# Feed-forward stages of a four-layer block: high weight blocks against both parts of the features in one 512-column product

## The chip, the cores and the metric

One core of one Trainium2 chip. The metric is the device time of one execution in microseconds (us). Engines: PE is TensorE (PEld its weight loads), DVE is VectorE, ACT is ScalarE, POOL is GpSimd, SP is the queue that issues the DMAs. The clock of TensorE has the levels 1.2 and 2.4 GHz.

## The reference, cut to what matters

Two blocks of two layers each run on 256 tokens of width 1024. The change concerns the feed-forward of the first block's two layers, with `D_FF = 2816`:

```python
def swiglu(h, w_in, w_out):
    a, b = jnp.split(h @ w_in, 2, axis=-1)
    return (jax.nn.silu(a) * b) @ w_out

def sandwich(x, mod, g_pre, g_post, fn):
    shift, scale, gate = mod
    h = rms_norm(x, g_pre) * (1.0 + scale[:, None]) + shift[:, None]
    return x + gate[:, None] * rms_norm(fn(h), g_post)
```

`mod` is the conditioning: `silu(c) @ ada_w + ada_b`, split in shift, scale and gate. After each feed-forward comes another mixer (dilated attention after the first, the second block's attention with an S5 scan after the second).

## The kernel before, in words

**Products in two parts.** All weights are float32. A weight piece of 128 x 1024 (512 KB) is split in a high part, rounded to fp32r (`WH`, made by ScalarE in `hi_to`, L1385), and a low part, the rest (`WL`, made by VectorE in `lo_to`, through the helper at L1876). Features are split likewise (`XH`, `XL`). A product is three matmuls, `mm3` (L633): high weight by high features (L634), and two with one low part each (L635, L636); low by low is left out. In the feed-forward's gate and up products the weight block (128x128) is the stationary operand and 256 tokens are the moving one.

**Pieces.** `weight_plan` lists 504 pieces in the order of use. SP loads them into four slots (`NRAW = 4`): piece n + 4 is loaded once piece n has its low part. Split parts have five slots (`NSPLIT = 5`). ScalarE and VectorE work `LOOK = 3` pieces ahead: `filled(u)` on either engine first makes the parts of all pieces up to `u.piece + LOOK` and then waits until TensorE has filled the unit `u`.

**A feed-forward stage** (`gated`) has 11 turns (`NF = 11`); turn i has a gate unit (2 pieces), an up unit (2 pieces), and the 2 down pieces of turn i - 1. A unit is 256 hidden features x 256 tokens, that is one PSUM bank of 512 columns. Piece numbers: the first feed-forward is 28 to 93, the second 134 to 199; in the second, turn i >= 1 has gate 132 + 6i and 133 + 6i, up 134 + 6i and 135 + 6i, down 136 + 6i and 137 + 6i. Gate and up units, and much else, take banks 0 to 3 (`PSA`) in a ring; the down products sum up in the four banks of `PSB`. After a unit, `gate` on ScalarE writes `Silu` of the bank to a buffer, `product` on VectorE multiplies it by the up bank, `high_of` (ScalarE, `GH`) and `low_of_product` (VectorE, `GL`) split the result for the down products.

**What stands beside it.** `ada_plan` and `ada_places` say behind which low part VectorE takes which step of the conditioning (40 steps in the first feed-forward, each 128 x 1024), before which piece TensorE sums over partitions (`ADA_TOTAL`, in `ada_total`, which takes one bank of the ring or two) and when its rows of `ada_w` are loaded. In the second feed-forward VectorE runs one step of `s5_setup` (a generator) behind each low part, from turn 2 on (`meanwhile` in `lo_to`); in turns 7 to 10 ScalarE takes one Abs and two Sin of 128 x 1024 between `gate` and `high_of`; and TensorE transposes small blocks in `s5_blocks` (two banks), which ScalarE copies to `AD`, in turns 5 and 9, between its `gate` and its `high_of`:

```python
for i in range(NF):
    gate(("ffn", 1), i)
    ...
    for k, where, dst in ((0, 5, BT), (1, 9, CTt)):
        if i == where:
            for r in range(2):
                u = ring.uses["s5t", k, r]
                filled(u)
                e.wait_ge(s_adastep.sem, ada_count(95))
                A.frees(e.copy(dst[r], v3(bank(u.b), 4)), u)
    ...
    high_of(("ffn", 1), i)
```

Every engine runs its program strictly in order. The first feed-forward runs from about 175 to 373 us, the second from about 570 to 760.

Of the kernel before, what the change touches and what calls it, by code (L numbers as in the profile page):

```python
# [7 lines left out]
ALU = mybir.AluOpType  # L8
ACTF = mybir.ActivationFunctionType
F32 = mybir.dt.float32  # L10
F32R = mybir.dt.float32r
# [3 lines left out]
P = 128  # L15
# [3 lines left out]
NF = 11  # L19
NRAW = 4  # L20
NSPLIT = 5
LOOK = 3
# [114 lines left out]
PLAN, FIRST = weight_plan()  # L137
# [26 lines left out]
def ada_plan():  # L164


    step, total, end = {}, {}, {}
    at = 1
    for p in range(2, 12):
        n, part = ADA_PARTS[p]  # L170
        if p == 5:
            at = FIRST["ffn", 0] + 2
        if p == 10:
            at = FIRST["att"] + 2
        pieces = {3: (12, 12, 13, 13, 16, 17, 17, 18), 4: (22, 22, 22, 22, 23, 24, 25, 26)}.get(p, range(at, at + 8))
        for k in range(8):
            if 8 * p + k not in ADA_BEHIND_LEVELS:
                step.setdefault(pieces[k], []).append(8 * p + k)
        last = pieces[7]
        if part == 2 and p != 3:  # L180
            last = max(last, FIRST[STAGES[n]] + ROWS_LOADED + 8)
        total[last + 1] = p
        if p != 3:
            end[last + (3 if p < 5 else 4)] = p
        at = last + (4 if p < 5 else 5)
    return step, total, end
# [174 lines left out]
def build(nc, a, out):  # L361
    ctx = ExitStack()
    with ctx:
        def sb(name, cols, dt=F32):
            return ctx.enter_context(nc.sbuf_tensor(name, [P, cols], dt))
# [11 lines left out]
        def sig(name):  # L377
            return Sig(ctx.enter_context(nc.semaphore(name)))

        PSA = ctx.enter_context(nc.psum_tensor("PSA", [P, 2048], F32))  # L380
        PSB = ctx.enter_context(nc.psum_tensor("PSB", [P, 2048], F32))
        XT = sb("XT", 2048)
        XH = sb("XH", 2048, F32R)
        XL = sb("XL", 2048, F32R)
        GHF = plain("GHF", 2048)
        GH = sb("GH", 2048, F32R)
        GLF = plain("GLF", 2048)
# [6 lines left out]
        T2 = sb("T2", 2048)  # L394
# [21 lines left out]
        s_sq, s_t2, s_xl, s_diag, s_mu = (sig(f"s_{n}_made") for n in ("sq", "t2", "xl", "diag", "mu"))  # L416
        s_xn, s_v, s_y, s_upd, s_fin = (sig(f"s_{n}_made") for n in ("xn", "v", "y", "upd", "fin"))
        s_gh, s_gl = sig("s_gh_made"), sig("s_gl_made")
        ring = Ring(0, [sig(f"s_bank{i}_filled").sem for i in range(4)], [sig(f"s_bank{i}_free").sem for i in range(4)])
# [15 lines left out]
            return CT[0:p, at + a0:at + a0 + n]  # L435

        ident, onesd = cst("ident"), cst("onesd")
        xh, xl = v3(XH[:, :], 8), v3(XL[:, :], 8)
        gh, gl = v3(GH[:, :], 8), v3(GL[:, :], 8)
        t2 = v3(T2[:, :], 8)  # L440
        junk, diag = T2[:, :], v3(T2[:, 1792:2048], 2)
# [5 lines left out]
        def bank(b, lo=0, hi=512, p=P, p0=0):  # L447
            t = PSA if b < 4 else PSB
            o = (b % 4) * 512
            return t[p0:p0 + p, o + lo:o + hi]  # L450

        def quarter(t, b):

            return t[:, 512 * b:512 * b + 512]

        def score_at(u, qt):

# [18 lines left out]
        def used(n):  # L476
            stage = sum(1 for x in ends if x <= n)
            if n + 1 in ends:
                return s_y.sem, 4 * (stage + 1)
            return s_used.sem, n + 1 - stage  # L480


        GLB, at = {}, 0
# [4 lines left out]
        STAGE = {n: i for i, n in enumerate(FIRST)}  # L488


        SPLIT = {n: i for i, n in enumerate(x for x in FIRST if x[0] != "moe")}
# [3 lines left out]
        r = Region(AR, 0, ARENA)  # L495
# [28 lines left out]
        r = Region(AR, 0, ARENA)  # L524
# [9 lines left out]
        blk = AR[:, 1024:2048]  # L534
# [9 lines left out]
        r = Region(AR, 0, ARENA)  # L544
# [9 lines left out]
        r = Region(ARR, 0, ARENA)  # L554
# [6 lines left out]
        r = Region(AR, r.at, 15376)  # L561
# [3 lines left out]
        eouts.append((ARR[:, r.at:r.at + 1024], ARR[:, r.at + 1024:r.at + 2048]))  # L565
        eraw = [r.take(1024) for _ in range(NFAR)]

        sm_at = [640]

        def small(n):  # L570
# [33 lines left out]
        s_glua, s_pad, s_conv, s_silu = (sig(f"s_{n}_made") for n in ("glua", "pad", "conv", "silu"))  # L604
        s_md, s_msb, s_mg, s_mh = (sig(f"s_{n}_made") for n in ("mdec", "msb", "mg", "mh"))
        s_open = sig("s_gates_open")
        s_rd, s_ra = sig("s_route_dve"), sig("s_route_act")
        s_s5r = sig("s_s5_read")
        s_ot, s_rx, s_glum, s_em = (sig(f"s_{n}_made") for n in ("ot", "route", "glum", "em"))
# [17 lines left out]
        def _(e):  # L627
            taken = [0]
# [45 lines left out]
            def half_of_features(u, half, stage):  # L674
                n, h, l = piece()
                h, l = v3(h, 4), v3(l, 4)
                for f in range(2):
                    for k in range(4):
                        kk = 4 * half + k
                        if n - FIRST[stage] < 2 and f == 0:  # L680
                            e.wait_ge(s_xl.sem, 8 * SPLIT[stage] + kk + 1)
                        t = mm3(bank(u.b, f * 256, f * 256 + 256), h[:, k, f * P:(f + 1) * P],
                                l[:, k, f * P:(f + 1) * P], xh[:, kk, :], xl[:, kk, :],
                                half == f == k == 0, kk == 7)
                t.then_inc(used(n)[0], 1)

            def features(tag, stage, free=None):
                u = use(tag, fill=used(taken[0] + 1), free=free)
                u.piece = taken[0] + 1
                half_of_features(u, 0, stage)  # L690
                half_of_features(u, 1, stage)

            def column(tag, stage):
                u = use(tag, fill=used(taken[0]))
# [166 lines left out]
            for f in range(8):  # L861
                t = mm(bank(shifts.b, f, f + 1), accs[1][:, f * P:(f + 1) * P], onesd[:, 0:1], False, f == 7, skip=True)
# [12 lines left out]
            for s in range(2):  # L875
                u = use(("pp", s))
                for x in range(2):
                    g = 2 * s + x
# [29 lines left out]
            u = use("cross")  # L908
# [36 lines left out]
            def gated(stage, n, aside):  # L945
                for i in range(n + 1):
                    if i < n:
                        features((stage, "g", i), stage)
                        aside(3 * i)
                        features((stage, "u", i), stage)  # L950
                        aside(3 * i + 1)
                    if i:
                        if i == 1:
                            aside(-1)
                            wait_sums_read(STAGE[stage])
                        for k in range(2):
                            down(2 * ((i - 1) % 2) + k, GLB[stage] + i, i == 1 and k == 0, i == n and k == 1)
                        aside(3 * i + 2)
# [68 lines left out]


            def s5_blocks(at):
                for k, (where, src) in enumerate(((15, lambda r, i: blk[:, r * 512 + i * P:r * 512 + i * P + P]),  # L1030
                                                  (27, lambda r, i: v4(blk, 2, 4)[:, r, i, :]))):
                    if at == where:
                        e.wait_ge(s_s5b.sem, 1 + k)
                        for r in range(2):
                            u = use(("s5t", k, r))
                            for i in range(4):
                                t = e.transpose(bank(u.b, i * P, i * P + P), src(r, i), ident)
                            t.then_inc(u.fill[0], 1)
# [329 lines left out]
        def _(e):  # L1368
# [3 lines left out]
            def act(o, i, f, bias=0.0, scale=1.0, accum=None):  # L1372
                if accum is None:
                    return e.activation(o, i, f, bias=bias, scale=scale)  # L1374
                return e.activation(o, i, f, bias=bias, scale=scale, accum_out=accum)  # L1375
# [144 lines left out]


            def gate(stage, i):
                u = ring.uses[stage, "g", i]
                filled(u)
                if i >= 2:
                    e.wait_ge(s_gl.sem, GLB[stage] + i - 1)
                A.frees(act(tmps[STAGE[stage]][i % 2], v3(bank(u.b), 2), ACTF.Silu), u)

            def high_of(stage, i):
                u = ring.uses[stage, "u", i]  # L1530
                hi_to(u.piece + LOOK)
                e.wait_ge(*u.free)
                if i >= 2:
                    sem, n = used(FIRST[stage] + 6 * (i - 2) + 9)
                    e.wait_ge(sem, n)
                A(e.copy(gh[:, 2 * (i % 2):2 * (i % 2) + 2, :], tmps[STAGE[stage]][i % 2]), s_gh)
# [325 lines left out]
        def _(e):  # L1862
# [12 lines left out]
            def tt(o, i, j, op):  # L1875
                return e.tensor_tensor(o, i, j, op)  # L1876
# [20 lines left out]
            def filled(u):  # L1897
                if u.piece >= 0:
                    lo_to(u.piece + LOOK)
                e.wait_ge(*u.fill)  # L1900
# [328 lines left out]


            def product(stage, i):
                u = ring.uses[stage, "u", i]
                filled(u)
                e.wait_ge(*ring.uses[stage, "g", i].free)
                tmp = tmps[STAGE[stage]][i % 2]
                V.frees(tt(tmp, tmp, v3(bank(u.b), 2), ALU.mult), u)

            def low_of_product(stage, i):
                low_of(GLB[stage] + i + 1, 2 * (i % 2), 2 * (i % 2) + 2, tmps[STAGE[stage]][i % 2])
# [774 lines left out]
```

## Time and profile before

| | us |
|---|---|
| three runs | 1496.88, 1496.77, 1500.34 |
| their median | 1496.88 |
| the profiled execution, its own time | 1494.02 |
| its span | 1492.1 |

```profile
span 1492.1 us, 23619 instructions
```

In profile lines `xN` is the number of instructions, `[... <-...]` the idle time before an instruction and what ended it, and matmul ends are modelled: how often TensorE can start one is read from the starts.

### The profile page before, as it was taken

To read this page: it belongs to the slowest core of one execution; us is meant where nothing else is said; L and a number is where in the kernel's file an instruction comes from. 1 tells how busy PE (TensorE), PEld (TensorE's weight loads), DVE (VectorE), ACT (ScalarE), POOL (GpSimd) and SP (SyncE) were. 2 spreads that over 40 slices of the span, in tenths; PEclk is the share of its full clock that TensorE was granted. 3 is DMA by queue.
4 is the path that set the end of the run, shared out by engine and by line. 5 is a ranking of instruction groups with operands and counts; after the bars stand their busy time and mean duration, and the time that the engine had idled before them with its cause. 6 is when DMAs were issued, how large, how long until landed. Compare 5 with 4: busy or idle time off the path is not lost.

```text
span 1492.1 us, 23619 instructions
## 1 busy us (share of the span) xinstructions
PE 1419.6 (95%) x9122; PEld 1267.0 (85%) x9122; DVE 1153.5 (77%) x1740; ACT 815.3 (55%) x1189; POOL 1.2 (0%) x5
## 2 busy tenths in 40 slices
PE   7989999999999999999999879999999999899997
PEld 7987899899998979999979768777879998787786
DVE  5998876875866646598569887799988966889997
ACT  2432443434443446444675436788866564678884
POOL 0000000000000000000000000000000000000000
PEclk8999999999999999999999999999999999999999
DMA  9983689986565513656734125899953535589992
GB/s 367 341 315 101 219 302 328 334 293 213 184 198 175 179 57 128 198 177 182 208 113 142 57 91 183 312 360 367 378 199 114 162 122 156 196 320 370 357 367 82
DMA packets 184483, 333.81 MB, mean 224 GB/s; under 512 B 13340, under 2 KB 127796, under 8 KB 184372
## 3 DMA queue, kind: packets, MB, share of 16 engines
q1 hardware_dynamic: 184372, 332.31, 64.7%
q8 instruction: 73, 1.20, 0.3%
q14 instruction: 38, 0.31, 0.1%
HBM read 331.18 MB, written 1.09 MB: 223 GB/s over the span
## 4 chain that ended last, share of the span: by engine, by line
PE 79%; DVE 12%; ACT 4%; issue 3%; DMA 1%; SPq 0%; ACTq 0%; DVEq 0%
PE PSA L634 17%; PE PSA L636 16%; PE PSA L635 16%; PE PSA L631 8%; PE PSB L634 6%; PE PSB L635 5%; PE PSB L636 5%; PE PSB L631 4%; DVE WL L1876 2%; DVE T L1876 2%; ACT WH L1385 1%; DVE ACC L1873 1%; DVE AR L1876 1%; ACT T L1375 1%; DMA WR<-hyb_w_in 1%
## 5 line engine op out<-in xcount | busy, mean ns | idle before, releaser
L1876 DVE TENSOR_TENSOR WL<-WR,WH 128x1024 fp32r<-128x1024 f32 x352 | 421.8, 1220 | 121.4 <-ACT WH L1385 120.8
L1385 ACT CAST WH<-WR 128x1024 fp32r<-128x1024 f32 x352 | 354.9, 1048 | 104.1 <-DMA WR<-hyb_w_in 44.9
L634 PE MATMUL PSA<-XH,WH 128*128 128x256 f32 x1312 | 378.7, 289 | 8.5 <-DVE AR L2278 2.5
L635 PE MATMUL PSA<-XL,WH 128*128 128x256 f32 x1312 | 372.6, 284 | 0.0
L636 PE MATMUL PSA<-XH,WL 128*128 128x256 f32 x1312 | 372.6, 284 | 0.0
L634 PEld LDWEIGHTS PSA<-XH,WH 128*128 128x128 f32 x1312 | 253.0, 193 | 13.5 <-issue 5.4
L635 PEld LDWEIGHTS PSA<-XL,WH 128*128 128x128 f32 x1312 | 253.1, 193 | 1.2 <-issue 0.7
L636 PEld LDWEIGHTS PSA<-XH,WL 128*128 128x128 f32 x1312 | 252.8, 193 | 0.0
L1876 DVE TENSOR_TENSOR WL<-AR,WH 128x1024 fp32r<-128x1024 f32 x152 | 178.4, 1220 | 18.8 <-ACT WH L1385 18.6
L634 PE MATMUL PSB<-WH,GH 128*128 128x512 f32 x416 | 164.7, 396 | 3.3 <-DVE GL L1876 3.3
L635 PE MATMUL PSB<-WL,GH 128*128 128x512 f32 x416 | 162.8, 391 | 0.0
L636 PE MATMUL PSB<-WH,GL 128*128 128x512 f32 x416 | 162.8, 391 | 0.0
L1385 ACT CAST WH<-AR 128x1024 fp32r<-128x1024 f32 x152 | 151.4, 1049 | 5.0 <-PE PSA L636 5.0
L634 PE MATMUL PSA<-WH,XH 128*128 128x256 f32 (+1 forms) x352 | 116.1, 330 | 5.5 <-DVE AR L1873 2.7
L1374 ACT ACTIVATE AR<-PSA 128x256 f32<-128x256 f32 (+1 forms) x82 | 37.7, 462 | 143.9 <-PE PSA L636 143.9
L636 PE MATMUL PSA<-WH,XL 128*128 128x256 f32 (+1 forms) x352 | 113.5, 322 | 0.0
L635 PE MATMUL PSA<-WL,XH 128*128 128x256 f32 (+1 forms) x352 | 113.2, 322 | 0.0
L634 PEld LDWEIGHTS PSB<-WH,GH 128*128 128x128 f32 x416 | 78.5, 189 | 22.2 <-issue 6.8
L636 PEld LDWEIGHTS PSB<-WH,GL 128*128 128x128 f32 x416 | 78.5, 189 | 16.8
L635 PEld LDWEIGHTS PSB<-WL,GH 128*128 128x128 f32 x416 | 78.5, 189 | 15.4 <-issue 0.2
L631 PE MATMUL PSA<-CT 128*128 128x256 f32 (+1 forms) x312 | 74.8, 379 | 7.0 <-DMA XT<-x 7.0
L634 PEld LDWEIGHTS PSA<-WH,XH 128*128 128x128 f32 x352 | 67.0, 190 | 11.7 <-DVE AR L1873 2.9
(259 smaller groups left out, 2042.4 us busy)
## 6 DMA issues: line engine op xcount, KB each, us to landing
AR<-moe_w_gate_up SPq DMA_DIRECT2D x96, 512.0 KB, 5.9
WR<-ffn_w_in SPq DMA_DIRECT2D x88, 512.0 KB, 4.5
WR<-moe_w_gate_up SPq DMA_DIRECT2D x64, 512.0 KB, 5.8
AR<-ada_w SPq DMA_DIRECT2D x59, 512.0 KB, 8.6
AR<-moe_w_down SPq DMA_DIRECT2D x56, 512.0 KB, 6.0
WR<-ffn_w_out SPq DMA_DIRECT2D x44, 512.0 KB, 4.3
WR<-att_w_qkv SPq DMA_DIRECT2D x36, 512.0 KB, 4.8
AD<-ada_w SPq DMA_DIRECT2D x34, 512.0 KB, 5.8
```

The costliest lines, as they stand in the source:

```text
L631: return e.matmul(o, l, r, start=start, stop=stop, skip_group_check=skip)
L634: e.matmul(o, lh, rh, start=start, stop=False, skip_group_check=True)
L635: e.matmul(o, lh, rl, start=False, stop=False, skip_group_check=True)
L636: return e.matmul(o, ll, rh, start=False, stop=stop, skip_group_check=True)
L1374: return e.activation(o, i, f, bias=bias, scale=scale)
L1375: return e.activation(o, i, f, bias=bias, scale=scale, accum_out=accum)
L1385: A(e.copy(hi_slot(m), raw_slot(m)), s_hi)
L1873: return e.scalar_tensor_tensor(out=o, in0=i, scalar=s, in1=j, op0=op0, op1=op1)
L1876: return e.tensor_tensor(o, i, j, op)
```

## The change

In all gate units and in the up units of turns 0 to 9, a high weight block meets the high and the low features in one matmul of 512 columns; the low block meets the high features in one of 256, added to the half for small sums. `XH` and `XL` become one tensor, `XHL`. A unit then takes two banks: for each of its two feature blocks, 256 columns of large sums and 256 of small ones. The last up unit keeps three matmuls and one bank. ScalarE copies the small sums out, VectorE adds the large ones; Silu then reads the buffer. ScalarE makes one high part more before it waits for VectorE. In `ada_plan` the steps and sums inside the first feed-forward move back by four pieces (the last by three), and the S5 transposes move from behind the gate unit of turns 5 and 9 (`aside` numbers 15, 27) to behind the down products in the same turns (17, 29).

```diff
 ada_plan:
-            at = FIRST["ffn", 0] + 2
+            at = FIRST["ffn", 0] + 6
...
-        pieces = {3: (12, 12, 13, 13, 16, 17, 17, 18), 4: (22, 22, 22, 22, 23, 24, 25, 26)}.get(p, range(at, at + 8))
+        pieces = {3: (12, 12, 13, 13, 16, 17, 17, 18), 4: (22, 22, 22, 22, 23, 24, 25, 26),
+                  9: (82, 83, 84, 85, 86, 87, 88, 88)}.get(p, range(at, at + 8))
 TensorE:
+            def wide_half(u, half, stage):
+                n, h, l = piece()
+                h, l = v3(h, 4), v3(l, 4)
+                for f in range(2):
+                    large_and_small = v3(bank(u.b + f), 2)
+                    for k in range(4):
+                        kk = 4 * half + k
+                        if n - FIRST[stage] < 2 and f == 0:
+                            e.wait_ge(s_xl.sem, 8 * SPLIT[stage] + kk + 1)
+                        mm(large_and_small, h[:, k, f * P:(f + 1) * P], xhl[:, :, kk, :], half == k == 0, kk == 7, skip=True)
+                        t = mm(large_and_small[:, 1, :], l[:, k, f * P:(f + 1) * P], xh[:, kk, :], False, kk == 7, skip=True)
+                t.then_inc(used(n)[0], 1)
+            def wide_features(tag, stage):
+                u = use(tag, 2, fill=used(taken[0] + 1))
...
-                        features((stage, "g", i), stage)
+                        wide_features((stage, "g", i), stage)
                         aside(3 * i)
-                        features((stage, "u", i), stage)
+                        (wide_features if i < n - 1 else features)((stage, "u", i), stage)
...
-                for k, (where, src) in enumerate(((15, ...), (27, ...))):
+                for k, (where, src) in enumerate(((17, ...), (29, ...))):
 ScalarE, gate:
-                A.frees(act(tmps[STAGE[stage]][i % 2], v3(bank(u.b), 2), ACTF.Silu), u)
+                A(e.copy(tmp, parts_of(u)[1]), s_small)
+                hi_to(u.piece + LOOK + 1)
+                e.wait_ge(*u.free)
+                A(act(tmp, tmp, ACTF.Silu), s_fsil)
 ScalarE, high_of:
                 hi_to(u.piece + LOOK)
-                e.wait_ge(*u.free)
+                if i < NF - 1:
+                    e.wait_ge(*u.fill)
+                    if nth:
+                        e.wait_ge(s_prod.sem, nth)
+                    A(e.copy(up_sum, parts_of(u)[1]), s_small)
+                    hi_to(u.piece + LOOK + 1)
+                    e.wait_ge(s_prod.sem, nth + 1)
+                else:
+                    e.wait_ge(*u.free)
 VectorE, product:
-                filled(u)
-                e.wait_ge(*ring.uses[stage, "g", i].free)
-                tmp = tmps[STAGE[stage]][i % 2]
-                V.frees(tt(tmp, tmp, v3(bank(u.b), 2), ALU.mult), u)
+                filled(g)
+                e.wait_ge(s_small.sem, smalls + 1)
+                V.frees(tt(tmp, parts_of(g)[0], tmp, ALU.add), g)
+                filled(u)
+                if i == NF - 1:
+                    e.wait_ge(s_fsil.sem, nth + 1)
+                    V.frees(tt(tmp, tmp, v3(bank(u.b), 2), ALU.mult), u)
+                else:
+                    e.wait_ge(s_small.sem, smalls + 2)
+                    V.frees(tt(up_sum, parts_of(u)[0], up_sum, ALU.add), u)
+                    e.wait_ge(s_fsil.sem, nth + 1)
+                    V.wait()
+                    V(tt(tmp, tmp, up_sum, ALU.mult), s_prod)
```

## Rows read from the trace of the kernel before

**Rows 1.** The page: busy time by engine, and the chain by engine.

```profile
PE 1419.6 (95%) x9122; PEld 1267.0 (85%) x9122; DVE 1153.5 (77%) x1740; ACT 815.3 (55%) x1189; POOL 1.2 (0%) x5
...
PE 79%; DVE 12%; ACT 4%; issue 3%; DMA 1%; SPq 0%; ACTq 0%; DVEq 0%
```

**Rows 2.** Windows, two turns of each stage: busy us (instructions), clock, DMA share, GB/s.

```profile
241.00:277.00 36.00, 36.00 (x254) 33.64 (x255) 23.18 (x24) 12.95 (x16) 0.00 (x0) 1.00 1.01 348
...
629.60:665.00 35.40, 35.40 (x248) 32.68 (x248) 32.63 (x52) 16.05 (x19) 0.00 (x0) 1.00 0.58 181
```

**Rows 3.** Timeline of TensorE, first feed-forward: start us, us, engine, line, operation.

```profile
209.77 0.28 PE L634 MATMUL PSA<-XH,WH 128*128 128x256 f32 x1
...
217.93 0.28 PE L636 MATMUL PSA<-XH,WL 128*128 128x256 f32 x1
218.05 0.40 PE L634 MATMUL PSB<-WH,GH 128*128 128x512 f32 x1
...
223.29 0.39 PE L636 MATMUL PSB<-WH,GL 128*128 128x512 f32 x1
223.51 0.28 PE L634 MATMUL PSA<-XH,WH 128*128 128x256 f32 x1
```

**Rows 4.** Timeline of TensorE, start of the up unit of turn 6.

```profile
283.86 0.28 PE L636 MATMUL PSA<-XH,WL 128*128 128x256 f32 x1
284.83 0.38 PE L634 MATMUL PSA<-XH,WH 128*128 128x256 f32 x1 [0.69 <-ACT AR L1374]
```

**Rows 5.** Timeline, start of the first feed-forward, ScalarE and TensorE.

```profile
172.38 3.75 ACT L1374 ACTIVATE T<-PSA,MC 128x256 f32<-128x256 f32 x8 [3.21 <-PE PSA L631]
...
175.16 0.36 PE L634 MATMUL PSA<-XH,WH 128*128 128x256 f32 x1
```

**Rows 6.** Timeline of VectorE, second feed-forward, turns 4 and 5.

```profile
640.91 1.22 DVE L1876 TENSOR_TENSOR WL<-WR,WH 128x1024 fp32r<-128x1024 f32 x1
...
649.56 0.68 DVE L1876 TENSOR_TENSOR AR<-AR,PSA 128x512 f32<-128x512 f32 x1
650.93 0.69 DVE L1876 TENSOR_TENSOR GL<-AR,GH 128x512 fp32r<-128x512 f32 x1 [0.69 <-ACT GH L1536]
651.88 1.22 DVE L1876 TENSOR_TENSOR WL<-WR,WH 128x1024 fp32r<-128x1024 f32 x1 [0.26 <-ACT WH L1385]
...
654.28 1.22 DVE L1876 TENSOR_TENSOR WL<-WR,WH 128x1024 fp32r<-128x1024 f32 x1
...
656.67 1.22 DVE L1876 TENSOR_TENSOR WL<-WR,WH 128x1024 fp32r<-128x1024 f32 x1
...
658.53 1.22 DVE L1876 TENSOR_TENSOR WL<-WR,WH 128x1024 fp32r<-128x1024 f32 x1
...
660.84 1.22 DVE L1876 TENSOR_TENSOR WL<-WR,WH 128x1024 fp32r<-128x1024 f32 x1
...
663.44 1.22 DVE L1876 TENSOR_TENSOR WL<-WR,WH 128x1024 fp32r<-128x1024 f32 x1
```

**Rows 7.** Timeline of TensorE, the transposes of turn 5.

```profile
656.62 1.04 PE L1037 MATMUL PSA<-CT,AR 128*128 128x128 f32 x8
657.41 0.36 PE L634 MATMUL PSA<-XH,WH 128*128 128x256 f32 x1
```

**Rows 8.** Timeline of ScalarE, turn 5: the copies of the transposes.

```profile
657.31 1.07 ACT L1590 COPY AD<-PSA 128x512 f32<-128x512 f32 x2
```

**Rows 9.** Timeline of ScalarE, turn 9: Abs and two Sin.

```profile
727.03 2.17 ACT L1374 ACTIVATE AR<-AR 128x1024 f32<-128x1024 f32 x2
729.12 1.13 ACT L1374 ACTIVATE AR<-AR,CT 128x1024 f32<-128x1024 f32 x1
```

**Rows 10.** Windows at a fall of TensorE's clock (columns as in rows 2).

```profile
776.90:780.30 3.40, 1.59 (x19) 1.02 (x18) 2.98 (x4) 2.06 (x6) 0.00 (x0) 1.00 0.13 14
780.30:783.80 3.50, 3.50 (x17) 3.50 (x18) 1.03 (x1) 3.37 (x8) 0.00 (x0) 0.51 0.87 286
```

More of the change, by code:

```diff
@@ L382, in build @@
         XT = sb("XT", 2048)
-        XH = sb("XH", 2048, F32R)
-        XL = sb("XL", 2048, F32R)
+        XHL = sb("XHL", 4096, F32R)
         GHF = plain("GHF", 2048)
@@ L437, in build @@
         ident, onesd = cst("ident"), cst("onesd")
-        xh, xl = v3(XH[:, :], 8), v3(XL[:, :], 8)
+        xhl = v4(XHL[:, :], 2, 8)
+        xh, xl = xhl[:, 0], xhl[:, 1]
         gh, gl = v3(GH[:, :], 8), v3(GL[:, :], 8)
@@ L454, in quarter, with parts_of @@
             return t[:, 512 * b:512 * b + 512]
+        def parts_of(u):
+            return tuple(v4(PSA[:, u.b * 512:u.b * 512 + 1024], 2, 2)[:, :, x] for x in range(2))
         def score_at(u, qt):
@@ L566, in build @@
         eraw = [r.take(1024) for _ in range(NFAR)]
+        up_sum = v3(T2[:, 1024:1536], 2)
         sm_at = [640]
@@ L606, in build @@
         s_open = sig("s_gates_open")
+        s_small, s_fsil, s_prod = (sig(f"s_ffn_{n}_made") for n in ("small", "silu", "product"))
         s_rd, s_ra = sig("s_route_dve"), sig("s_route_act")
@@ L691, in features @@
                 half_of_features(u, 1, stage)
+            def wide_half(u, half, stage):
[12 more added lines that the diff above has]
+                u = use(tag, 2, fill=used(taken[0] + 1))
+                u.piece = taken[0] + 1
+                wide_half(u, 0, stage)
+                wide_half(u, 1, stage)
             def column(tag, stage):
@@ L1029, in s5_blocks @@
             def s5_blocks(at):
-                for k, (where, src) in enumerate(((15, lambda r, i: blk[:, r * 512 + i * P:r * 512 + i * P + P]),
-                                                  (27, lambda r, i: v4(blk, 2, 4)[:, r, i, :]))):
+                for k, (where, src) in enumerate(((17, lambda r, i: blk[:, r * 512 + i * P:r * 512 + i * P + P]),
+                                                  (29, lambda r, i: v4(blk, 2, 4)[:, r, i, :]))):
                     if at == where:
@@ L1522, in gate @@
             def gate(stage, i):
-                u = ring.uses[stage, "g", i]
+                u, tmp = ring.uses[stage, "g", i], tmps[STAGE[stage]][i % 2]
                 filled(u)
@@ L1526, in gate @@
                     e.wait_ge(s_gl.sem, GLB[stage] + i - 1)
-                A.frees(act(tmps[STAGE[stage]][i % 2], v3(bank(u.b), 2), ACTF.Silu), u)
+                A(e.copy(tmp, parts_of(u)[1]), s_small)
+                hi_to(u.piece + LOOK + 1)
+                e.wait_ge(*u.free)
+                A(act(tmp, tmp, ACTF.Silu), s_fsil)
             def high_of(stage, i):
-                u = ring.uses[stage, "u", i]
+                u, nth = ring.uses[stage, "u", i], (NF - 1) * (STAGE[stage] // 2) + i
                 hi_to(u.piece + LOOK)
-                e.wait_ge(*u.free)
+                if i < NF - 1:
[7 more added lines that the diff above has]
+                    e.wait_ge(*u.free)
                 if i >= 2:
@@ L2231, in product @@
             def product(stage, i):
-                u = ring.uses[stage, "u", i]
-                filled(u)
-                e.wait_ge(*ring.uses[stage, "g", i].free)
-                tmp = tmps[STAGE[stage]][i % 2]
-                V.frees(tt(tmp, tmp, v3(bank(u.b), 2), ALU.mult), u)
+                g, u, tmp = ring.uses[stage, "g", i], ring.uses[stage, "u", i], tmps[STAGE[stage]][i % 2]
+                nth, smalls = NF * (STAGE[stage] // 2) + i, (2 * NF - 1) * (STAGE[stage] // 2) + 2 * i
+                filled(g)
+                e.wait_ge(s_small.sem, smalls + 1)
+                V.frees(tt(tmp, parts_of(g)[0], tmp, ALU.add), g)
+                filled(u)
+                if i == NF - 1:
[7 more added lines that the diff above has]
+                    V(tt(tmp, tmp, up_sum, ALU.mult), s_prod)
             def low_of_product(stage, i):
```

## The prediction

> **What bounds the kernel now.** I read the page's first and fourth parts, then the two feed-forward stages stage by stage. TensorE is busy 95% of the span and carries 79% of the chain that ended last, VectorE 12% [rows 1]. So a product saved on TensorE is time saved, provided that the split weight blocks and the PSUM banks still come in time. The windows say where that is in doubt: the first feed-forward's two turns at 241 have VectorE busy 23.2 us of 36, with DMA at its limit, while in the second's two turns at 630 VectorE is busy 32.6 of 35.4 [rows 2]. TensorE hardly waits in either.
>
> **The products.** TensorE starts a matmul of 256 columns every 0.120 us (68 steps in 8.16 us) and one of 512 every 0.228 (23 steps in 5.24); going from 256 to 512 costs 0.12, from 512 to 256 0.22 to 0.23: the cost is that of the earlier matmul [rows 3]. A weight block of 128x128 costs 3 x 0.120 = 0.360 now, and 0.228 + 0.120 = 0.348 afterwards: 0.0125 us less. What goes is one matmul's fixed part, not streaming. There are 21 wide units per stage (11 gate, 10 up) of 16 blocks: 336, two stages 672, so 8.4 us, 4.2 in each stage. No row shows a moving operand in two strips of 256, 2048 columns apart; I take the plain 0.228, its nearest row. The bounds: 0.240 (as two narrow ones: gain 0), and both matmuls at bare streaming, 512/2.4 + 256/2.4 = 0.320 a block (gain 26.9 us).
>
> Here a rule speaks otherwise. The Trainium skill, TensorE: Matmul & The Clock Gate (Back-to-back issue gap), gives N/2.4 + 2.5 ns between matmuls for a single stream; 512 and 256 columns would then take 0.216 + 0.109. By it, with now's 0.360 kept, 672 blocks would save 23.5 us. The trace doesn't agree: beyond streaming it has 13 to 14 ns for either width.
>
> **First feed-forward (pieces 28 to 93).** A unit now needs two of four banks. Gate, up, gate, up use the pairs in turn, so a unit waits for the one two before it, which has 11 us to be read. The moved conditioning sums (pieces 42, 54, 66, 78, 89 in place of 38, 50, 62, 74, 86) come after both units of a turn, so no up unit lands on its own gate's banks. That happens once now, at 283.86: 0.97 us between matmuls, 0.85 of it a wait for ScalarE's Silu [rows 4]. I count -0.85. VectorE gets two additions of 0.69 more per turn, ScalarE two copies of 0.60; of VectorE's 13 us of slack per two turns [rows 2] this takes 2.8, so 0. The conditioning DMAs move four pieces with their sums, on SP past the bias table's load; fewer stand ahead of that load, one or two stand between it and the same weights as before: 0, bounds -1 and +2 (DMA share 1.01). At the stage's start the first gate waits for the features' transposes 5 and 6 to be read, now only for 4. ScalarE's eight reads run from 172.38 for 3.75, so number 6 ends at about 175.7; TensorE started at 175.16 [rows 5]: +0.55, and +0.1 in the second stage, where the ring stands one bank otherwise. First stage: -4.2 - 0.85 + 0.55 = -4.5.
>
> **Second feed-forward (pieces 134 to 199): VectorE's chain.** The S5 set-up runs in steps behind each low split (the line that writes WL). From WL of piece 160 at 640.91 to the end of that of 163 at 653.10 VectorE has only the wait of 0.69 for GH and 0.26 for WH [rows 6]: 12.2 us. Afterwards this stretch has two additions (+1.4), and the 0.26 goes, as ScalarE splits one piece ahead: 13.3. It starts some 1.3 earlier, at 639.6 (TensorE is 1.5 us ahead by gate 3, ScalarE splits 156 directly after its short S5 work, one addition more stands before), and ends at 653.0; bounds 0.8 either way. TensorE wanted piece 163 at 653.74 (656.62 less 24 x 0.12, [rows 7]), a margin of 0.65. By then 21 halves have saved 0.10 each: wanted at 651.65, wait 1.3.
>
> From there VectorE sets the pace. A gate's addition stands behind the low splits up to three pieces on, and Silu waits for it. I step on with 2.40 from a split to the next over a long set-up step, 1.87, 2.31 and 2.60 over others [rows 6], 1.7 over two short ones (estimate), 0.7 for an addition, 2.06 from product to end of GL; TensorE with 2.78 a half unit and 2.73 a down piece.
> - Turn 5: 164 starts at 654.2, 165 at 656.6, 166 at 658.5, gate 5's addition at 660.8, 167 at 661.5, 168 at 664.1. TensorE does 163 from 653.0, is through up 5 at 661.4 and the down products at 666.85. Then the wait at gate 6 (next part); WL 169 ends at 673.1.
> - Turn 6: 170 at 674.3, 171 at 676.7, 172 at 678.6, gate 6's addition 680.9, 173 at 681.6, 174 at 684.2, up 6's addition 686.6, WL 175 ends at 690.6. TensorE, from 673.1, wants it after a half, up 6, two down pieces and a half: 689.7. Wait 0.9.
> - Turn 7: gate 7 is full at 694.1, but its addition comes behind 176, 177 and 178 at 697.5. Now Silu follows TensorE at once; then it starts at 698.2, Abs and two Sin behind it, and high split 180 begins at 701.9. So 181's low split ends at 709.2, wanted at 707.2: wait 2.0.
> - Turn 8: in the same way 1.4 at 186 and 1.1 at 187.
>
> Together 1.3 + 0.9 + 2.0 + 1.4 + 1.1 = 6.7 us.
>
> **The S5 transposes.** They move from pieces 164 and 188 to 168 and 192: from behind gate 5 (and 9) to behind up 5 (9) and the down products. ScalarE's program doesn't move with them. It runs gate(5), then the copies of the transposes, then high_of(5), which now begins with the copy of up 5's small sums. So ScalarE waits for transposes that come after the down products; up 5's copy is queued behind that wait; VectorE waits for the copy; and gate 6 needs the banks of up 5, with nothing between the transposes and it. TensorE's 0.79 us of transposes stands either way [rows 7]. Then it waits for two copies (1.07, [rows 8]), the small copy (half of that and its end, 0.60), the addition (0.68, as the product in [rows 6]) and handoffs (0.25, an estimate), less 0.4 that the first copy overlaps: 2.2 us. Its second piece, WL 169, comes 3.3 later (product, GH, GL in 2.06, a split in 1.22) against a half unit's 2.78: 0.5. In turn 9 Abs and two Sin (3.1, [rows 9]) stand between the copies and the small copy: 2.2 + 3.1 = 5.3, and 0.5 again. Sum 8.5. VectorE idles beside both; the chain above counts that in. Nothing hides these waits, as all other work of TensorE is ordered behind gate 6 and gate 10.
>
> The clock: it fell to 1.2 GHz for 3.5 us (granted 0.51) after a stretch with TensorE busy 1.59 of 3.40 us [rows 10]. A wait of 5.3 is emptier, so I expect one fall: up to 1.7 us, less 0.5 that the late split 193 covers: +1.2, bounds 0 and 3.4 (both waits).
>
> **Sum.** -8.4 - 0.85 + 0.65 + 6.7 + 8.5 + 1.2 = +7.8 us. The profiled execution took 1494.02 (span 1492.1), so 1501.8 by its own time; the median of the runs shown, 1496.88, is 2.86 above it, and I give the result on that: 1504.7 us. The attention stage gets other bank numbers but the same order of reuse: 0.
>
> **Rivals.**
> - Only the S5 waits bite; VectorE's chain keeps its lead (its steps overlap better than I add them). -8.6 + 8.5 + 1.2 = +1.1: 1498. For: they are ordering, not throughput. Against: a margin of 0.65 us and 92% busy. Chance 0.20.
> - Faster: VectorE keeps its lead and the four-bank ring doesn't hold TensorE in turns 5 and 9, because ScalarE's copy of the small sums doesn't wait there as I read it. It decides at gates 6 and 10: if TensorE starts them within 0.3 us of the transposes, only -8.6 is left: 1488. Chance 0.08.
> - The 512 columns cover the next weight load, and only streaming is left: 0.320 a block. The second stage ends by VectorE's chain, which doesn't move, so the first alone gains, 336 x 0.040 = 13.4 in place of 4.2; the waits stay. +7.8 - 9.2 = -1.4: 1495.5. For: the 0.012 beyond streaming at 256 could be the load of 128 columns. Against: the same stands behind 512. Chance 0.07. The gap that the Trainium skill gives on the page above is this case with 11.8 for 13.4.
> - Nothing gained: two strips cost as two matmuls (0.240). Second stage as forecast, first 4.2 worse: +12: 1509. Or DMA holds the first stage or both waits drop the clock: +10 to +12. Chance 0.12.
> - The forecast, +4.5 to +10: 0.53.
>
> **The numbers.** About 0.3%, 4.5 us, is what a measurement of this kernel can tell from no change. Faster by more: the second rival and a little of the third, 0.10. Within: the first, most of the third and the forecast's lower edge, 0.28. Slower: 0.62. The range leaves out the fast case and the worst of the fourth: 1494 to 1511.
>
> **What would show it.** Spacing of 0.228 and 0.120 in turn within a wide unit; no bank wait in the first stage, which ends 4 to 5 us earlier. In the second, low splits just before or after TensorE wants them from turn 5 on; TensorE idle 2.2 us at gate 6 and 5.3 at gate 10, put down to VectorE's addition; a clock drop there. I am wrong if TensorE runs through gates 6 and 10, or if the second stage isn't longer than now.

## The result and the profile after

| us | before | after |
|---|---|---|
| median (lowest to highest), five runs each | 1496.88 (1496.54 to 1500.34) | 1508.56 (1506.52 to 1513.03) |
| the profiled execution, its span | 1494.02, 1492.1 | 1513.03, 1511.2 |
| first feed-forward, first gate product to last down product | 197.93 | 194.95 |
| between the two | 196.72 | 198.12 |
| second feed-forward | 190.33 | 203.45 |
| from there to TensorE's last matmul | 722.73 | 722.68 |

Slower: ratio 1.0074, interval 1.0058 to 1.0089, 11.7 us by the medians; +7.8 was forecast. The stage lengths are worked out from the starts of the TensorE instructions; those of the two feed-forward stages include 0.23 for the last product, the two other rows run from start to start. The first feed-forward gained 3.0 us and the second lost 13.1. The two profiled executions also differ by 7.5 us ahead of the first feed-forward (it starts at 182.69, before at 175.16) and by 1.4 between the two, where the change touches little or nothing; before_again, below, comes back to that. So stages are compared here, not ends of span.

The page of the changed kernel: span, busy times, the chain by engine, and the group of the new product, to be read beside [rows 1].

```profile
span 1511.2 us, 22426 instructions
...
PE 1426.0 (94%) x8450; PEld 1240.5 (82%) x8450; DVE 1179.4 (78%) x1782; ACT 840.0 (56%) x1231; POOL 1.2 (0%) x5
...
PE 66%; DVE 18%; ACT 6%; issue 5%; DMA 4%; SPq 1%; ACTq 0%; DVEq 0%
...
L640 PE MATMUL PSA<-XHL,WH 128*128 128x512 f32 x672 | 241.3, 402 | 12.0 <-DVE T L1917 7.1
```

672 matmuls fewer, and TensorE is no less busy; its share of the chain fell from 79 to 66%, VectorE's rose from 12 to 18%. The group's last numbers are the loss in short: 12 us of idle time before the wide matmuls, 7.1 of it ended by VectorE's addition of the sums.

The timeline of TensorE in the first stage (start, length, instruction) answers to [rows 3], and its lines at 284 to [rows 4].

```profile
217.72 0.40 PE L640 MATMUL PSA<-XHL,WH 128*128 128x512 f32 x1
217.96 0.28 PE L640 MATMUL PSA<-XHL,WL 128*128 128x256 f32 x1
...
222.31 0.40 PE L640 MATMUL PSA<-XHL,WH 128*128 128x512 f32 x1
...
284.72 0.28 PE L640 MATMUL PSA<-XHL,WL 128*128 128x256 f32 x1
285.82 0.50 PE L640 MATMUL PSA<-XHL,WH 128*128 128x512 f32 x1 [0.82 <-DVE WL L1917]
```

From 217.72 to 222.31 are 13 pairs, 353 ns each. Over the whole stage, by the recorded starts, the next matmul starts 234.5 ns behind a wide one and 116.7 behind a narrow one on average, 351 a block (the medians are 233 and 117, but the steps behind a wide one vary from 230 to 241, so the average is what adds up). The wait for a bank is gone, but TensorE waits 0.98 us at 284.72, now for a low part. VectorE's timeline:

```profile
283.93 0.69 DVE L1917 TENSOR_TENSOR GL<-AR,GH 128x512 fp32r<-128x512 f32 x1 [0.69 <-ACT GH L1577]
284.54 1.22 DVE L1917 TENSOR_TENSOR WL<-WR,WH 128x1024 fp32r<-128x1024 f32 x1
```

The high part that this split needs was ready at 282.17 (ScalarE's copy of 1.05 from 281.12); the split stood behind the product and `GL` in VectorE's program.

The timeline at gates 6 and 10, TensorE first. The transposes are L1067; an `xN` line holds N instructions, the last of which start at 673.96 and 749.24.

```profile
673.20 1.04 PE L1067 MATMUL PSA<-CT,AR 128*128 128x128 f32 x8
676.24 0.50 PE L640 MATMUL PSA<-XHL,WH 128*128 128x512 f32 x1 [2.01 <-DVE T L1917]
...
748.47 1.04 PE L1067 MATMUL PSA<-CT,AR 128*128 128x128 f32 x8
754.58 0.80 PE L640 MATMUL PSA<-XHL,WH 128*128 128x512 f32 x1 [5.07 <-DVE T L1917]
755.17 0.42 PE L640 MATMUL PSA<-XHL,WL 128*128 128x256 f32 x1
755.39 0.63 PE L640 MATMUL PSA<-XHL,WH 128*128 128x512 f32 x1
755.82 0.41 PE L640 MATMUL PSA<-XHL,WL 128*128 128x256 f32 x1
756.03 0.63 PE L640 MATMUL PSA<-XHL,WH 128*128 128x512 f32 x1
```

ScalarE and VectorE in the same two places: copies of the transposes (L1631), Abs and Sin (L1404), the copy of the small sums (L1569), then VectorE's addition (L1917, `T<-PSA,T`).

```profile
673.83 1.07 ACT L1631 COPY AD<-PSA 128x512 f32<-128x512 f32 x2 [2.67 <-PE PSA L1067]
674.79 0.60 ACT L1569 COPY T<-PSA 128x512 f32<-128x512 f32 x1
675.50 0.69 DVE L1917 TENSOR_TENSOR T<-PSA,T 128x512 f32<-128x512 f32 x1 [2.98 <-ACT T L1569]
...
749.11 1.07 ACT L1631 COPY AD<-PSA 128x512 f32<-128x512 f32 x2 [2.42 <-PE PSA L1067]
750.07 2.16 ACT L1404 ACTIVATE AR<-AR 128x1024 f32<-128x1024 f32 x2
752.13 1.13 ACT L1404 ACTIVATE AR<-AR,CT 128x1024 f32<-128x1024 f32 x1
753.17 0.56 ACT L1569 COPY T<-PSA 128x512 f32<-128x512 f32 x1
753.84 0.69 DVE L1917 TENSOR_TENSOR T<-PSA,T 128x512 f32<-128x512 f32 x1 [9.11 <-ACT T L1569]
```

Read from the end: TensorE waits for the addition, that for the small copy, that for ScalarE's place in its program behind the transposes' copies, and those for transposes that now come last in the turn. ScalarE stood idle 2.67 and 2.42 us with up 5's and up 9's small sums ready.

Windows around the two waits (columns as in [rows 2]).

```profile
673.80:677.20 3.40, 1.39 (x9) 1.07 (x8) 1.39 (x2) 1.74 (x4) 0.00 (x0) 1.00 0.07 25
677.20:680.60 3.40, 3.40 (x13) 2.82 (x12) 2.90 (x3) 2.34 (x3) 0.00 (x0) 0.50 0.04 6
745.50:752.30 6.80, 4.01 (x22) 3.19 (x20) 0.00 (x0) 4.21 (x6) 0.00 (x0) 1.00 0.29 101
752.30:759.10 6.80, 4.52 (x14) 3.85 (x15) 4.48 (x6) 3.95 (x5) 0.00 (x0) 0.50 0.04 9
```

The clock was granted at 0.50, the 1.2 GHz level, twice: from 677.2 for 3.4 us, 1.0 us after TensorE had resumed at 676.24, and from 752.3 for 6.8 us, of which the first 2.3 lie still in the wait that ended at 754.58. In a fall a pair takes 0.64 us (755.39 to 756.03, above). Summed over the matmuls, the falls cost 1.5 and 2.1 us.

The waits between engines in the second feed-forward (engine, line, waited for: us, times, longest):

```profile
PE PSA L640 <- DVE T L1917: 7.1, 2, 5.1
ACT AD L1631 <- PE PSA L1067: 5.1, 2, 2.7
...
PE PSA L640 <- DVE WL L1917: 3.7, 4, 1.1
```

### The profile page after: what moved, and what is told of

The parts are those of the page before. It is cut to its first block, busy times and chain, and to the rows that moved or that the text cites. A ratio compares the mean times of both kernels' runs of the same rounds, so it can differ in the third digit from the quotient of the medians.

```text
span 1511.2 us, 22426 instructions
## 1 busy us (share of the span) xinstructions
PE 1426.0 (94%) x8450; PEld 1240.5 (82%) x8450; DVE 1179.4 (78%) x1782; ACT 840.0 (56%) x1231; POOL 1.2 (0%) x5
## 4 chain that ended last, share of the span: by engine, by line
PE 66%; DVE 18%; ACT 6%; issue 5%; DMA 4%; SPq 1%; ACTq 0%; DVEq 0%
PE PSA L640 16%; PE PSA L643 11%; PE PSA L645 10%; PE PSA L644 10%; DVE WL L1917 5%; PE PSB L643 4%; PE PSB L645 4%; PE PSB L644 4%; PE PSB L640 4%; DVE T L1917 3%; DMA WR<-ffn_w_in 2%; ACT WH L1415 2%; DVE AR L1917 2%; DVE ACC L1914 2%; DMA WR<-hyb_w_in 1%
## 5 line engine op out<-in xcount | busy, mean ns | idle before, releaser
L1917 DVE TENSOR_TENSOR WL<-WR,WH 128x1024 fp32r<-128x1024 f32 x352 | 422.0, 1218 | 80.0 <-ACT WH L1415 79.3
L1415 ACT CAST WH<-WR 128x1024 fp32r<-128x1024 f32 x352 | 358.7, 1048 | 119.1 <-DMA WR<-hyb_w_in 44.5
L640 PE MATMUL PSA<-XHL,WH 128*128 128x512 f32 x672 | 241.3, 402 | 12.0 <-DVE T L1917 7.1
L643 PE MATMUL PSA<-XHL,WH 128*128 128x256 f32 x640 | 187.8, 294 | 7.2 <-ACT T L1404 2.2
L1917 DVE TENSOR_TENSOR WL<-AR,WH 128x1024 fp32r<-128x1024 f32 x152 | 178.3, 1218 | 19.3 <-ACT WH L1415 19.3
L640 PE MATMUL PSA<-XHL,WL 128*128 128x256 f32 x672 | 190.0, 283 | 0.0
L644 PE MATMUL PSA<-XHL,WH 128*128 128x256 f32 x640 | 183.3, 286 | 0.0
L645 PE MATMUL PSA<-XHL,WL 128*128 128x256 f32 x640 | 183.2, 286 | 0.0
L640 PEld LDWEIGHTS PSA<-XHL,WH 128*128 128x128 f32 x672 | 127.9, 190 | 44.8 <-DVE T L1917 7.6
L643 PEld LDWEIGHTS PSA<-XHL,WH 128*128 128x128 f32 x640 | 124.9, 195 | 11.1 <-issue 5.2
L640 PEld LDWEIGHTS PSA<-XHL,WL 128*128 128x128 f32 x672 | 128.6, 191 | 0.6
L644 PEld LDWEIGHTS PSA<-XHL,WH 128*128 128x128 f32 x640 | 125.0, 195 | 0.5 <-issue 0.5
L645 PEld LDWEIGHTS PSA<-XHL,WL 128*128 128x128 f32 x640 | 124.9, 195 | 0.0
L643 PE MATMUL PSA<-WH,XHL 128*128 128x256 f32 (+1 forms) x352 | 116.1, 330 | 6.3 <-DVE AR L1914 2.7
L645 PE MATMUL PSA<-WH,XHL 128*128 128x256 f32 (+1 forms) x352 | 113.4, 322 | 0.0
L644 PE MATMUL PSA<-WL,XHL 128*128 128x256 f32 (+1 forms) x352 | 113.2, 322 | 0.0
```

The lines of the kernel that those rows point to most:

```text
L640: return e.matmul(o, l, r, start=start, stop=stop, skip_group_check=skip)
L643: e.matmul(o, lh, rh, start=start, stop=False, skip_group_check=True)
L644: e.matmul(o, lh, rl, start=False, stop=False, skip_group_check=True)
L645: return e.matmul(o, ll, rh, start=False, stop=stop, skip_group_check=True)
L1415: A(e.copy(hi_slot(m), raw_slot(m)), s_hi)
```

## The experiments

The theory is that of the prediction: ScalarE's order makes the waits at gates 6 and 10, VectorE's chain the four others. The rivals are that the waits are VectorE's throughput, whatever the order; and, for the size of the gain, that the two strips of the 512 columns cost time.

**again**, the changed kernel unchanged.

> The changed kernel once more, for a second profile. In the first one the hybrid stage, which the change doesn't touch, stood 5.3 us later than in the profile before, and the stages from piece 28 on 13.8. If that 5.3 is spread between executions and not the change, this profile has another value there and the same lengths of the feed-forward stages: 195 us for the first (F start to last down product) and 203.5 for the second. If the change causes it, it is there again. Time: 1506 to 1511.

1509.96 us (1504.76 to 1512.76, six runs) against 1497.86 (28 runs of before): 1.0081, interval 1.0062 to 1.0100. Waits at gates 6 and 10 of 2.17 and 5.24 us; for low parts 0.93, 1.20, 1.25 and 0.92; the clock fell at 676.2 and 751.3. First stage 194.57, second 203.99, between 198.02: the waits lie in the same places and are the same to 0.1 us.

**s5_behind.** The transposes stay where the change put them; ScalarE's program moves with them.

```diff
-                (copies of the S5 transposes, turns 5 and 9)
                 if i >= 7:
                     (Abs, two Sin)
                 high_of(("ffn", 1), i)
+                (copies of the S5 transposes, turns 5 and 9)
```

> One edit: ScalarE copies the S5 transposes behind high_of in turns 5 and 9 instead of ahead of it. Theory (ScalarE's order holds up 5 and up 9): TensorE no longer waits at gates 6 and 10 (2.2 and 5.2 us now), no clock fall behind them (some 4 us), the second stage 10 to 12 us shorter: 192 to 194 us, whole kernel 1497 to 1499. Rival (VectorE's load is what delays it): the waits at low splits grow by what the gates lose, and the stage stays above 199. Second rival (the ring of two-bank units makes TensorE wait there in any order): both waits stay.

1498.84 us (12 runs), ratio 1.0005, interval 0.9991 to 1.0020. Second stage 193.06, 10.4 us shorter. Its timeline, ScalarE (small copy first, transposes' copies L1638 behind) and TensorE:

```profile
663.76 0.58 ACT L1569 COPY T<-PSA 128x512 f32<-128x512 f32 x1
...
670.15 1.06 ACT L1638 COPY AD<-PSA 128x512 f32<-128x512 f32 x2
```

```profile
667.92 1.03 PE L1067 MATMUL PSA<-CT,AR 128*128 128x128 f32 x8
668.71 0.48 PE L640 MATMUL PSA<-XHL,WH 128*128 128x512 f32 x1
...
740.12 1.04 PE L1067 MATMUL PSA<-CT,AR 128*128 128x128 f32 x8
740.91 0.48 PE L640 MATMUL PSA<-XHL,WH 128*128 128x512 f32 x1
```

Gates 6 and 10 start right behind the transposes, and the lower clock was granted at no moment of the stage. That is shown, then: with the transposes in their new place, the two waits come from the order of ScalarE's program, and both falls go with them. The low parts are still late: 0.93 (piece 163), 0.34 (175), 1.88 (181), 1.38 (186), 0.93 (187), 5.5 us in all.

**no_long_steps.** The changed kernel without the 12 VectorE steps of 128 x 1024 that subtract the parts of the angles' period in the S5 set-up (this part of the angles' reduction is left out).

```diff
-                    (12 times, in the angles' reduction)
-                    V.wait()
-                    V(stt(x, n, -c, x, ALU.mult, ALU.add))
```

> The changed kernel without three of the four long steps of each S5 angle reduction: 12 scalar_tensor_tensor of 1.22 us on VectorE in turns 4 to 8 are left out (the angles are then not reduced, only clipped). Theory: the waits for low splits at pieces 163, 181, 186, 187 (0.93, 1.25, 1.24, 0.93 us, 4.35 in sum) go, those at gates 6 and 10 stay at 2.2 and 5.2 and the clock falls too: second stage 198.5 to 199.5 us, kernel 4 to 5 us below the changed one. Rival (VectorE's load is the cause of all): the gate waits go as well, 10 us or more.

1502.47 us (9 runs), ratio 1.0033, interval 1.0019 to 1.0048; second stage 197.75. The waits at gates 6 and 10 stay at 2.17 and 5.24 us; the four waits for low parts, 4.35 us, are gone. A new one of 0.38 stands at 677.07, at the second piece of gate 6. So the first two are no matter of VectorE's throughput, the others are. Its waits in the stage:

```profile
ACT AD L1631 <- PE PSA L1067: 9.5, 2, 4.8
PE PSA L640 <- DVE T L1917: 7.1, 2, 5.1
...
PE PSA L640 <- DVE WL L1917: 0.2, 1, 0.2
```

The stage came out shorter than expected, as "the clock falls too" held only in part. Windows over and behind the wait at gate 6 (it ended at 674.25), and one over the end of that at gate 10 (748.14) and what follows:

```profile
671.40:674.80 3.40, 1.39 (x11) 1.11 (x10) 1.19 (x2) 1.56 (x3) 0.00 (x0) 1.00 0.00 0
674.80:678.20 3.40, 3.19 (x18) 2.53 (x17) 2.71 (x4) 2.52 (x3) 0.00 (x0) 1.00 0.00 0
...
747.80:751.20 3.40, 3.06 (x9) 2.67 (x10) 2.61 (x4) 2.28 (x3) 0.00 (x0) 0.50 0.00 0
```

The same wait at gate 6 had no fall behind it here, the one at gate 10 a fall of 3.4 us in place of 6.8. Of the 5.7 us by which the stage is shorter, some 2 belong to the clock and not to VectorE's steps: the fall costs 1.5 us here, the two of the changed kernel 3.6.

**s5_behind_short**, both edits together.

> s5_behind with the 12 long steps of the angle reduction left out too (angles only clipped). If the gate waits (ScalarE's order) and the waits at low splits (VectorE's load) are the only costs of the second stage, both are gone together, and the products' 10 ns a pair stand alone: 190.3 - 3.4 = 187 us. If the stage stays above 189, a third cost is open.

One run: 1492.45 us, no wait and no fall left in the second stage, 187.72 us: 2.6 less than before's 190.33. The gain of the products shows as soon as nothing else holds them. It is not the 3.4 expected: 336 blocks at 351 ns in place of 360 are 2.9, and the down products, which the change leaves as they were, take 0.3 more (229.0 ns from one to the next in place of 227.9).

**first_only.** Wide units in the first feed-forward alone; the second as before, with the transposes at their old place.

```diff
-                        wide_features((stage, "g", i), stage)
+                        (wide_features if stage[1] == 0 else features)((stage, "g", i), stage)
...
-                for k, (where, src) in enumerate(((17, ...), (29, ...))):
+                for k, (where, src) in enumerate(((15, ...), (27, ...))):
```

> Wide products in the first feed-forward alone; the second has the three narrow matmuls, one bank per unit and the old places of the transposes. Theory: the first stage as in the changed kernel (195 us against 197.9), the second as before (190.3), start of the stage 0.6 later: 2.4 us below the kernel before, ratio 0.998. If the two strips or the shared tensor cost anything elsewhere, the ratio is 1.000 or more.

1495.93 us (12 runs), ratio 0.9993, interval 0.9981 to 1.0005; first stage 194.54, second 190.33. The whole loss sits in the second stage. The stage's gain of 3.4 us is in the profile; the total shows 1.9 less than before by the medians (1.0 by the ratio) and can't be told from no change.

**before_again**, the kernel before once more, to learn what between the profiles is not the change's.

> The kernel before once more, for a second profile: where TensorE's clock falls in it (101, 145 and 780 us in the first profile, none at 470) and how long its stages are. In four profiles of changed kernels a fall of 3.4 us stood at 467 to 472 and the attention stage was 1.1 to 1.3 us longer. If that belongs to the moment a stage is reached and not to the change, this profile may have it too, with the feed-forward stages at 197.9 and 190.3 again.

1498.75 us. The first feed-forward starts at 178.29 (175.16 in the first profile), the middle takes 198.15 (196.72), the two feed-forwards 198.10 and 190.33, as they did. The clock falls at other moments than in the first profile (147.7 and 472.0 us). So the 1.4 us between the stages and 3.1 of the 7.5 us ahead of the first one are spread between executions of one kernel. The other 4.4 are in the main the same: the changed kernel and those variants of it whose programs differ from it only in the second feed-forward start the first at 177.78 (early_add), 177.98 (s5_behind), 181.55 (both_behind) and 182.69. About 0.6 are the change's own (the start, below).

**contiguous.** `XHL` laid out block by block, so that the moving operand is one strip.

```diff
-        xhl = v4(XHL[:, :], 2, 8)
+        xhl = v4(XHL[:, :], 8, 2)
...
-                        mm(large_and_small, ..., xhl[:, :, kk, :], ...)
+                        mm(large_and_small, ..., xhl[:, kk, :, :], ...)
```

> The changed kernel with the shared feature tensor laid out by block, large and small next to each other, so that the wide product's moving operand is one strip of 512 columns. Theory (reading two strips costs the 6 ns by which the wide product is longer than other 512-column ones): start to start 227 after the wide and 120 after the narrow one, 347 a pair in place of 350, 1 us less in the first stage (193.5). Rival (the 233 and 117 come from the change of width): the pair stays at 350.

One run: 1509.51 us. Six pairs from its timeline of TensorE, first stage:

```profile
213.67 0.40 PE L640 MATMUL PSA<-XHL,WH 128*128 128x512 f32 x1
213.91 0.28 PE L640 MATMUL PSA<-XHL,WL 128*128 128x256 f32 x1
...
215.79 0.40 PE L640 MATMUL PSA<-XHL,WH 128*128 128x512 f32 x1
```

2.12 us for six, 353 ns a pair as in the changed kernel's row of 13; over the first stage 234.4 and 116.8 on average, against 234.5 and 116.7. The two strips cost nothing; that rival falls. The waits at gates 6 and 10 are the same again (2.17 and 5.23 us), and each has a fall of 3.4 us behind it.

**both_behind.** As s5_behind, and Abs and Sin of turns 7 to 10 behind `high_of` too.

```diff
-                if i >= 7:
-                    (Abs, two Sin)
                 high_of(("ffn", 1), i)
                 (copies of the S5 transposes)
+                if i >= 7:
+                    (Abs, two Sin)
```

> ScalarE copies the S5 transposes and takes the Abs and two Sin of turns 7 to 10 behind high_of instead of ahead of it. Theory (in turns 7 and 8 the high splits 180 and 186 stand behind 3.1 us of Abs and Sin, and these behind VectorE's late addition): against s5_behind the waits at 181 (1.88), 186 (1.38) and 187 (0.93) shrink to under 1.5 in sum; second stage 190 to 191 us in place of 193.1, kernel 1495 to 1497. Rival (VectorE's own load sets these waits): they stay, 193.

1495.19 us (12 runs), ratio 0.9981, interval 0.9970 to 0.9992; second stage 189.55. Of the waits for low parts 0.94 (163) and 0.45 (175) are left; those of 181, 186 and 187, 4.2 us, are gone. ScalarE's timeline in turn 9: GH (L1577) and a split go ahead of the copies (L1632) and of Abs and Sin (L1404).

```profile
737.61 0.62 ACT L1577 CAST GH<-AR 128x512 fp32r<-128x512 f32 x1 [0.67 <-DVE AR L1917]
738.14 1.04 ACT L1415 CAST WH<-WR 128x1024 fp32r<-128x1024 f32 x1
741.34 1.08 ACT L1632 COPY AD<-PSA 128x512 f32<-128x512 f32 x2 [2.16 <-PE PSA L1067]
742.30 2.17 ACT L1404 ACTIVATE AR<-AR 128x1024 f32<-128x1024 f32 x2
```

So these three waits needed two things: VectorE's long steps (no_long_steps lost them) and ScalarE's 3.1 us ahead of `high_of` (this kernel lost them).

**grouped.** both_behind with, for each block of features, two wide matmuls, then two narrow ones, so that widths change half as often.

```diff
-                for f in range(2):
-                    for k in range(4):
-                        (wide matmul of f, k; narrow matmul of f, k)
+                for k in range(4):
+                    for f in range(2):
+                        (wide matmul of f, k)
+                    for f in range(2):
+                        (narrow matmul of f, k)
```

> both_behind with the matmuls of a wide half unit in another order: for each of four feature blocks the two wide ones, then the two narrow ones, so that the width changes half as often and a narrow matmul does not add to the columns that the matmul just before it wrote. Forecast by what costs the 3 ns a pair beyond 227 + 120: the change of width or the same columns twice running: four matmuls take 694 to 697 ns in place of 700, 0.5 to 1 us less in the first stage (194.0 in place of 194.9), time 0.1% below both_behind. Rival (the 3 ns belong to any such pair): 700, no change.

1493.55 us (12 runs, one of them 7912.19, the others 1487.65 to 1499.67), ratio 0.9975, interval 0.9959 to 0.9992. The four matmuls of two blocks (lines x2, timeline of TensorE) start 233, 233, 116 and 116 ns apart on average over the stages, 698 together; in both_behind two pairs take 704:

```profile
217.71 0.62 PE L640 MATMUL PSA<-XHL,WH 128*128 128x512 f32 x2
218.18 0.40 PE L640 MATMUL PSA<-XHL,WL 128*128 128x256 f32 x2
218.41 0.63 PE L640 MATMUL PSA<-XHL,WH 128*128 128x512 f32 x2
```

So the order matters: 3 ns a block, and the first stage is 193.85 us for a forecast of 194.0 (both_behind 194.89), the second 188.49 (189.55). That is what was forecast for "the change of width or the same columns twice running"; which of the two it is, this run doesn't separate. That a wide matmul still takes 233 and not 228 behind another wide one is open. It is the fastest version that ran, faster than before by 0.25%; over both_behind it has 0.0006 by the ratios, which the intervals don't separate.

**early_add.** both_behind with the addition of the gate's sums before the low parts two and three pieces on, so that Silu starts earlier; the price is a later low part.

```diff
-                filled(g)
+                if stage[1]:
+                    lo_to(g.piece + 1)
+                    e.wait_ge(*g.fill)
+                else:
+                    filled(g)
```

> both_behind with VectorE's addition for a gate unit in the second stage ahead of the low splits two and three pieces on, instead of behind them. Theory (the addition's place delays Silu and all behind it on ScalarE): the waits at 163 (0.94) and 175 (0.45) don't come from that, but from VectorE's sum of work, and stay within 0.5 in sum; second stage 189.5 as now, at best 188.5. Rival (the order inside VectorE's chain sets them): both go, 188.1. A cost is possible too: where VectorE is not behind, it waits for the gate unit with two splits undone, and the low splits come late: over 190.5.

1497.58 us (12 runs), ratio 1.0003, interval 0.9990 to 1.0015. The waits grew to 2.07 (163), 0.70 (175) and 0.45 (181), the stage to 192.13: the price came, the profit did not. VectorE waits in its program for the gate unit while it could split: in the 82.9 us from the stage's start to shortly before the wait at 163 it is busy 57.4 us, in both_behind 58.5.

## Why the prediction was right, and where its sizes were off

The direction and its causes were right, and the time, 1508.56, lies in the range, 3.9 us above the number given. Term by term:

- **Products, -8.4: mis-sized, by 2.6.** 351 ns a block on average, not 348, against 360: 9 ns less, 2.9 us a stage, 5.8 in all. The step that failed took 0.228 and 0.120, each from a row of matmuls of one width; in turn they are 0.2345 and 0.117. (Its own two figures give 0.012 a block and 8.1; 8.4 takes 0.0125.) The second stage gained 2.6 us when unhindered. Neither end of the bounds came near. The gap that the Trainium skill gives for isolated matmuls on TensorE: Matmul & The Clock Gate (Back-to-back issue gap) would be 0.325 a pair, an estimate by that page; the runs have 0.351.
- **Bank wait, -0.85: right, but nothing came of it.** It went, and a wait of 0.98 (0.45 to 0.97 in other profiles) for a low part came near the same moment. I had counted VectorE at 0 in this stage, by its slack over two turns. The slack was there, but not at that moment: the split stood behind the product and `GL` in VectorE's program, 2.4 us after its high part was ready. The DMAs, for which I had given bounds of -1 and +2, don't end that wait.
- **Start, +0.55 and +0.1: right,** 0.62 and 0.16. From the first of the 32 transposes to the first gate product are 3.56 us before (171.60 to 175.16) and 4.18 after (178.51 to 182.69), in the second stage 3.57 and 3.72. This lies ahead of the stages as they are measured here.
- **S5 transposes, 2.2 and 5.3: right,** 2.17 and 5.23. The 0.5 after each, for the second piece, did not come: behind both waits the clock was lower, and TensorE asked for that piece later. In no_long_steps, where no fall came at gate 6, it is there, with 0.38.
- **VectorE's chain, +6.7: 4.35.** Measured 0.93, 0, 1.25, 1.24, 0.93 for 1.3, 0.9, 2.0, 1.4, 1.1. Where no clock fell (s5_behind) it is 5.5, with 1.88 and 1.38 where 2.0 and 1.4 stood; so 1.1 of the difference of 2.35 comes with the waits and falls that this kernel doesn't have. I put it down to the fall after gate 6, which took 1.5 us of TensorE's time and none of VectorE's; that is argued, not shown.
- **Clock, +1.2: mis-sized, by 2.4.** I expected one fall of 3.5 us, as in [rows 10]. Here there were two, the second of 6.8 us: 3.6 us together, a little over the bound of 3.4. "A wait of 5.3 is emptier" was the reason given for one fall. The same two waits had falls of 3.4 and 6.8 us in again, 3.4 and 3.4 in contiguous, none and 3.4 in no_long_steps: one fall was possible, and the length of a wait alone doesn't settle it.
- Not counted: the first matmul behind a wait takes 0.08 to 0.11 us longer to make way for the next, 0.5 us over five of the waits.

Second stage: -2.9 + 4.35 + 7.4 + 3.6 + 0.5 = 12.95 of 13.1 measured. My own sum for it was -4.2 + 6.7 + 8.5 + 1.2 = 12.2. That the two are close is luck: the waits were put 3.5 us too high, and the products, the clock and the first matmuls 4.2 too low. In the first stage the gain is 3.0 for a forecast of 5.05 (4.5 with the start). The two stages give +10.1 us and the two starts +0.8, together +10.9 for +11.7 by the medians; again gives +11.1 and +12.1. The 0.8 to 1.0 us between them lie outside both stages, where executions of one kernel spread by more, and stay open.

The measured +11.7 is above the forecast's own band of 4.5 to 10, where the fourth rival stood: its "both waits drop the clock" happened, "nothing gained" did not. The first rival (VectorE keeps its lead) has 4.35 us against it, the second (gates 6 and 10 run through) 7.4; the third would need 0.320 a block, and there are 0.351.

## What to carry to other kernels

A step moved on one engine has to be moved in the program of every engine that reads its result: each engine takes its work in order, and a consumer left in its old place holds up everything behind it. Here that cost 10 us, more than the 6 or so that 672 matmuls fewer brought, and moving a few lines gave it back. And before a stage's TensorE work is cut, see how far ahead the engines that feed it are: with VectorE busy 32.6 of 35.4 us the cut turned into waits, until ScalarE's unhurried work went behind the hurried.

## What was not expected of the hardware

- A matmul of 512 columns takes 228 ns among its like and more in this product: 233 to 236 on average in the stages of the profiles where it alternates with one of 256, in one strip or two, and 233 in twos. One of 256 takes 120 among its like, 117 alternating and 116 in twos. What adds up is 350 to 353 ns a block in turn, mostly 351, and 349 in twos.
- Behind a wait of TensorE of 2.2 us the lower clock came in three profiles (for 3.4 us) and not in a fourth; at one of 5.2 us it came in all four, for 6.8 us in two and 3.4 in two. The single waits of 0.9 to 1.25 us in this stage had none behind them, nor had those of 1.88 (s5_behind) and 2.07 (early_add).
- Two profiles of the same kernel have their clock falls at other moments (before: 145.4 or 147.7, and 472.0 in one alone), and with them stage lengths of 196.72 or 198.15 us. A difference of 1.4 us between two profiles in a stage that a change doesn't touch says nothing.
